# Samples' B and C in the state-space scan: spread over partitions by the tensor engine, or by a transfer through DRAM

## The reference

```python
state_new = state * exp(dt * a) + (dt * x)[:, None] * B[None, :]      # per head: 64 x 128
y = (state_new * C[None, :]).sum(-1) + d_skip * x
```

## Time and profile before

| | |
|---|---|
| median of 3 runs | 1481.87 us |
| profiled execution, its own time | 1483.19 us |
| its span in the trace | 1481.4 us |
| PE busy | 1396.4 us (94%) |
| DVE busy | 858.4 us (58%) |
| ACT busy | 568.1 us (38%) |
| POOL busy | 608.5 us (41%) |
| mean granted clock of TensorE | 0.97 |
| moved by DMA | 160.47 MB, mean 108 GB/s |

### The profile page before, as it was taken

The page is one execution under the profiler, slowest core; times in us unless marked ns, Lnnn a source line. Parts: engine busy times, 40 slices in busy tenths (PEclk is TensorE's granted clock), DMA queues, the critical chain, the costliest instruction groups (busy, mean ns, idle before and its releaser), DMA issues.

```text
span 1481.4 us, 28721 instructions
## 1 busy us (share of the span) xinstructions
PE 1396.4 (94%) x11570; PEld 1301.2 (88%) x11570; DVE 858.4 (58%) x1713; ACT 568.1 (38%) x1162; POOL 608.5 (41%) x753
## 2 busy tenths in 40 slices
PE   4998999999999999999999999999489999999994
PEld 4997898998989889898898877899479999999994
DVE  6477878878788787887876534233542222222226
ACT  3344544544545354444445222222233322233221
POOL 4442352433525335352423322445435454544541
PEclk9999999999999999999999999899779999999997
DMA  4222222322222232232334899433012223232231
GB/s 160 86 79 89 83 79 72 103 90 81 85 89 89 86 92 76 86 94 72 93 113 119 253 358 356 143 130 101 29 57 89 94 90 100 86 98 89 86 100 58
DMA packets 109588, 160.47 MB, mean 108 GB/s; under 512 B 16496, under 2 KB 83568, under 8 KB 109456
## 3 DMA queue, kind: packets, MB, share of 16 engines
q1 hardware_dynamic: 54864, 127.32, 27.2%
q10 hardware_dynamic: 54592, 31.33, 7.2%
HBM read 145.87 MB, written 12.74 MB: 107 GB/s over the span
## 4 chain that ended last, share of the span: by engine, by line
PE 66%; DVE 15%; ACT 4%; SPq 3%; issue 2%; DMA 1%; POOL 1%; ACTq 0%; DVEq 0%; POOLq 0%
PE lin L523 52%; SPq L400 2%; PE lin L730 2%; DVE arena L1528 1%; PE Pb L685 1%; PE Pb L556 1%; PE lin L626 1%; DVE arena L1691 1%; DVE ysum L1694 1%; ACT arena L1173 1%; PE Pb L669 1%; DVE sm L1613 1%; DMA w_stage<-in_wall 1%; PE Pb L678 1%; DVE arena L1621 1%
## 5 line engine op out<-in xcount | busy, mean ns | idle before, releaser
L471 POOL TENSOR_TENSOR w_lo<-w_stage,w_hi 128x256 fp32r<-128x256 f32 x736 | 587.7, 830 | 815.9 <-ACT w_hi L968 815.9
L523 PE MATMUL lin<-act_hi,w_hi 128*128 128x260 f32 x1760 | 367.1, 290 | 12.4 <-DVEq L1693 4.3
L523 PE MATMUL lin<-act_lo,w_hi 128*128 128x260 f32 x1760 | 357.0, 285 | 0.0
L523 PEld LDWEIGHTS lin<-act_hi,w_hi 128*128 128x128 f32 x1760 | 274.1, 191 | 26.9 <-issue 22.0
L523 PEld LDWEIGHTS lin<-act_lo,w_hi 128*128 128x128 f32 x1760 | 275.4, 191 | 0.0
L968 ACT ACTIVATE w_hi<-w_stage 128x1024 fp32r<-128x1024 f32 x184 | 193.5, 1052 | 200.2 <-PE lin L523 154.7
L523 PE MATMUL lin<-act_hi,w_lo 128*128 128x260 f32 x1760 | 236.0, 287 | 0.0
L523 PEld LDWEIGHTS lin<-act_hi,w_lo 128*128 128x128 f32 x1760 | 222.3, 191 | 0.0
L523 PE MATMUL lin<-mid_hi,w_hi 128*128 128x260 f32 x1008 | 206.5, 286 | 1.1 <-issue 1.1
L523 PE MATMUL lin<-mid_lo,w_hi 128*128 128x260 f32 x1008 | 203.9, 284 | 0.0
L523 PEld LDWEIGHTS lin<-mid_hi,w_hi 128*128 128x128 f32 x1008 | 157.6, 191 | 2.7 <-issue 2.3
(11 more groups left out here) (265 smaller groups left out, 1879.0 us busy)
## 6 DMA issues: line engine op xcount, KB each, us to landing
w_stage<-in_wall SPq DMA_DIRECT2D x184, 512.0 KB, 3.6
arena<-in_cache ACTq DMA_DIRECT2D x80, 144.0 KB, 4.4
arena<-in_state ACTq DMA_DIRECT2D x16, 512.0 KB, 5.1
out_stateT<-arena ACTq DMA_DIRECT2D x16, 512.0 KB, 4.1
o_attn<-in_cache SPq DMA_DIRECT2D x64, 128.0 KB, 4.3
arena<-in_cache SPq DMA_DIRECT2D x64, 128.0 KB, 4.1
arena<-in_cache SPq DMA_DIRECT2D x48, 144.0 KB, 4.2
arena<-in_xT SPq DMA_DIRECT2D x8, 520.0 KB, 5.5
```

The costliest lines, as they stand in the source:

```text
L471: low = pool.tensor_tensor(w_lo[:, slot, part], w_stage[:, slot, part], w_hi[:, slot, part].bitcast(F32), ALU.subtract)
L523: mm = pe.matmul(lin[:, pl.slot, hf, 0:HALF], w[:, ch.slot, off:off + P], r[:, hf * HALF:(hf + 1) * HALF], start=(k == 0 and p == 0), stop ...
```

## The change

B and C of the samples no longer pass through the tensor engine. DVE copies the 8 sample columns of `xc` (128 partitions x 8) into a small tile `smp` (`samples_apart`); ACT's queue writes it to a DRAM buffer of [8, 128], which takes one 4-byte piece for each of 1024 numbers (`samples_out`); when that has landed, ACT's queue reads the 4 KB back to each of the 128 partitions (`samples_in`), B into `sga_mid`, C into a part of the convolution's buffer. DVE waits for `b_in` and `c_in` and takes both operands of its products from SBUF. The entries bB and bC leave the list of slots. B and C of group i's inputs are written and read back at the end of group i; those of group 0 are read back in block 0 of group 1, where the state update now stands after `raw_samples(1)`, `sample_y(0)` after `scan_back(0)` and `sample_y(1)` in block 1.

```diff
--- before.py
+++ after.py
@@ -50,12 +50,12 @@
 S_LIN = [f"s{m}" for m in range(8)]
 FIRST_LIN = ["x0", "x1", "bcq", "b", "c", "bckv", "z0", "z1", "uq0", "uq1", "uk", "uv", "ql"]
 FIRST_CONV = [3, 0, 1, 2]
-STEADY_LIN = (["bB", "x0", "sA0", "x1", "bC", "sA1", "b", "sA2", "c", "sA3", "z0", "z1", "uq0", "uq1", "uk", "uv", "ql"]
+STEADY_LIN = (["x0", "sA0", "x1", "sA1", "b", "sA2", "c", "sA3", "z0", "z1", "uq0", "uq1", "uk", "uv", "ql"]
               + S_LIN)
 EARLY = 6
 OA_ORDER = [0, 1, 2, 3, 4, 7, 5, 6]
 OA_BEFORE = [0, 2, 4, 5, 6]
-LAST_LIN = (["bB", "ga0", "sA0", "ga1", "bC", "sA1", "ga2", "sA2", "ga3", "sA3", "ga4", "ga5", "ga6"] + S_LIN)
+LAST_LIN = (["ga0", "sA0", "ga1", "sA1", "ga2", "sA2", "ga3", "sA3", "ga4", "ga5", "ga6"] + S_LIN)
 FIRST_CH = IN_LIN + ["UQ", "UKV"]
 STEADY_CH = IN_LIN + ["UQ", "UKV", "SA", "SB"]
 LAST_CH = [f"ga{k}" for k in range(EARLY + 1)] + ["SA", "SB"]
@@ -121,7 +121,7 @@
     return fixed(CH_D + GATES_BEFORE[b] + q)
 
 
-C_LIN = [FIRST_LIN, ["x0", "bB"] + STEADY_LIN[2:]] + [STEADY_LIN] * 6 + [LAST_LIN]
+C_LIN = [FIRST_LIN] + [STEADY_LIN] * 7 + [LAST_LIN]
 
 
 def c_lin(i, name):
...
+    sdec_mm sdec_ready st_in0 st_in1 st_scaled smp_ready smp_out0 smp_out1 b_in c_in st_new st_out0 st_out1 scores max_bias exp_done prob_ready
...
@@ -235,6 +235,7 @@
         snb = sb("snb", [P, 3])
         sga_mid = sb("sga_mid", [P, 2, T])
         sm = sb("sm", [P, 8])
+        smp = sb("smp", [P, 2, NB])
         sms = sb("sms", [P, 8])
         ahead = sb("ahead", [SSM_HEADS, 1])
 
@@ -270,7 +271,7 @@
         sz = part(4 * T, "p (k t) -> p k t", k=4)
         yT = part(2 * T, "p (k t) -> p k t", k=2)
         state = part(256)
-        sT = arena[:, at[0]:at[0] + 2048].rearrange("p (t b n) -> p t b n", t=2, b=NB)
+        sT = arena[:, at[0]:at[0] + 1024].rearrange("p (b n) -> p b n", b=NB)
         sqg = arena[:, at[0]:at[0] + 2 * T].rearrange("p (k t) -> p k t", k=2)
         seg = part(512, "p (h l) -> p h l", h=HPG)
         ecs = part(512, "p (h l) -> p h l", h=HPG)
@@ -323,6 +324,13 @@
         sq2 = part(KT * T, "p (k t) -> p k t", k=KT)
         relu = part(2 * T + 68)[:, 68:].rearrange("p (k t) -> p k t", k=2)
         sqsum = part(T, "p (k t) -> p k t", k=1)
+
+        sT_first = o_attn[:, 6:8, :].rearrange("p k t -> p (k t)").rearrange("p (b n) -> p b n", b=NB)
+        B_all = sga_mid[:, :, :].rearrange("p k t -> p (k t)")[:, 0:NB * STATE]
+
+        def C_all(g):
+            a = early + 2 * T if g == GROUPS - 1 else early + 2 * T - 4 * CONVW + NB * STATE
+            return arena[:, a:a + NB * STATE]
 
         def sz_of(i, k):
             return sz[:, 2 * (i % 2) + k, :]
@@ -721,28 +729,15 @@
                     pe.wait_ge(S["cs_split"], 1)
                     first_scores()
                     project(0)
-                pe.wait_ge(S["xc_ready"], g * 4 + 4)
-
-                def on_all(name, k):
-                    pl = c_lin(i, name)
-                    free_slot(pl)
-                    for b in range(NB):
-                        mm = pe.matmul(lin[:, pl.slot, b // 4, (b % 4) * P:(b % 4 + 1) * P],
-                                       xc[:, k, SAMP0 + 4 * b:SAMP0 + 4 * b + 1].to_broadcast([P, P]), ident[:, :],
-                                       start=True, stop=True)
-                    mm.then_inc(S["lin_done"], 1)
-
-                on_all("bB", 2)
                 if g:
                     first_scores()
                     project(0)
+                pe.wait_ge(S["xc_ready"], g * 4 + 4)
                 for c in range(NCH):
                     u = 2 * c
                     scan_front(c)
                     scores(u + 1)
                     project(c + 1, between=lambda: transposes(u))
-                    if c == 0:
-                        on_all("bC", 3)
                     values(u)
                     transposes(u + 1)
                     scan_back(c)
@@ -1073,6 +1068,19 @@
                         scaled = act.activation(sS[:, t, b, :], sS[:, t, b, :], ACT.Identity,
                                                 scale=sdec_all[:, i, t, 8 + b:9 + b])
                     scaled.then_inc(S["st_scaled"], 1)
+
+                def samples_out(t):
+                    act.wait_ge(S["smp_ready"], i * 2 + t + 1)
+                    act.dma_start(o["samples"][i, t].rearrange("b n -> n b"), smp[:, t, :], allow_slow_non_contiguous=True).then_inc(S[f"smp_out{t}"], 16)
+
+                def samples_in(t, i=i):
+                    act.wait_ge(S[f"smp_out{t}"], i * 16 + 16)
+                    if t == 0:
+                        act.wait_ge(S["st_new"], i * 2)
+                    else:
+                        act.wait_ge(S["xc_ready"], i * 4 + 4)
+                    act.dma_start((B_all, C_all(i))[t], o["samples"][i, t].rearrange("b n -> (b n)").partition_broadcast(P)
+                                  ).then_inc(S[("b_in", "c_in")[t]], 16)
 
                 def queries_out(h):
                     pl = c_lin(i, f"uq{h}")
@@ -1132,6 +1140,8 @@
                     conv_tanh(2)
                     conv_tanh(3)
                     act.wait_ge(S["rows_ready"], 1)
+                    for t in range(2):
+                        samples_out(t)
                     return
 
                 def exponent(u):
@@ -1166,6 +1176,9 @@
                         act.wait_ge(S["state_ready"], g * 4 + c)
                     act.activation(Brow[:, :], lin[:, pl.slot, 1, 256:384], ACT.Copy).then_inc(S["a_row"], 1)
                     exponent(u + 1)
+                    if i == 1 and c == 0:
+                        for t in range(2):
+                            samples_in(t, 0)
                     act.wait_ge(S["a_seg"], g * 4 + (c + 1))
                     act.activation(ecs[:, :, :], lin[:, pl.slot, 0, :].rearrange("p (h l) -> p h l", h=HPG),
                                    ACT.Exp).then_inc(S["a_ecs"], 1)
@@ -1238,7 +1251,12 @@
                     conv_tanh(3)
                     scaled_state(0)
                     scaled_state(1)
+                    samples_out(0)
                 round_chunk(c_chunk(i, "SB").next())
+                if has_in:
+                    samples_in(0)
+                    samples_out(1)
+                    samples_in(1)
 
             group(0)
             for i in range(1, GROUPS):
@@ -1535,6 +1553,13 @@
                     dve.wait_ge(S["conv_tanh"], i * 4 + (n + 1))
                     dve.scalar_tensor_tensor(xc[:, k, :], xc[:, k, :], 1.0, cacc[:, k, :], ALU.add, ALU.mult
                                              ).then_inc(S["xc_ready"], 1)
+                    if has_rest and k >= 2:
+                        samples_apart(k - 2)
+
+                def samples_apart(t):
+                    dve.wait_ge(S[f"smp_out{t}"], i * 16)
+                    dve.wait_ge(S["xc_ready"], i * 4 + (3 + t if has_rest else 4))
+                    dve.tensor_copy(smp[:, t, :], xc[:, 2 + t, SAMP0:CONVW:4]).then_inc(S["smp_ready"], 1)
 
                 def queries_out(h):
                     pl = c_lin(i, f"uq{h}")
@@ -1605,6 +1630,8 @@
                     conv(3)
                     silu(2)
                     silu(3)
+                    samples_apart(0)
+                    samples_apart(1)
                     return
 
                 def row_max(u):
@@ -1666,31 +1693,27 @@
                 if g == 0:
                     row_max(0)
                     raw_samples(0)
-                dve.wait_ge(S["xc_ready"], g * 4 + 4)
-                dve.wait_ge(S["st_scaled"], g * 2 + 2)
-                link(dve.tensor_tensor(dtx[:, :, :], sdec_all[:, g, :, 0:8], xc[:, 0:2, SAMP0:CONVW:4], ALU.mult))
-                pl = c_lin(i, "bB")
-                bB = lin[:, pl.slot, :, :].rearrange("p a (b n) -> p (a b) n", b=4)
-                done(pl)
-                link(dve.tensor_tensor(sT[:, 0], bB, spread(dtx[:, 0, :], STATE), ALU.mult))
-                dve.tensor_tensor(sT[:, 1], bB, spread(dtx[:, 1, :], STATE), ALU.mult).then_inc(S["lin_free"], 1)
-                dve.wait_ge(S["lin_free"], pl.index + 1)
-                for t in range(2):
-                    dve.tensor_tensor(sS[:, t], sS[:, t], sT[:, t], ALU.add).then_inc(S["st_new"], 1)
-                    dve.wait_ge(S["st_new"], g * 2 + (t + 1))
+
+                def sample_states():
+                    dve.wait_ge(S["xc_ready"], g * 4 + 4)
+                    dve.wait_ge(S["st_scaled"], g * 2 + 2)
+                    link(dve.tensor_tensor(dtx[:, :, :], sdec_all[:, g, :, 0:8], xc[:, 0:2, SAMP0:CONVW:4], ALU.mult))
+                    dve.wait_ge(S["b_in"], g * 16 + 16)
+                    for t in range(2):
+                        new = sT if g else sT_first
+                        link(dve.tensor_tensor(new, B_all.rearrange("p (b n) -> p b n", b=NB), spread(dtx[:, t, :], STATE),
+                                               ALU.mult))
+                        dve.tensor_tensor(sS[:, t], sS[:, t], new, ALU.add).then_inc(S["st_new"], 1)
```

(23 more changed lines are left out.)

1 line of the change is left out of this document (removed).

## The result

The kernel after takes 1606.91 us (median of 4 runs, 1601.97 to 1609.84) against 1482.38 for the kernel before, measured with it: ratio 1.0835 [1.0814, 1.0856], slower by some 124 us. The forecast was 1489, in a range that ended at 1508. The direction was right and the size far off. The profiled execution of after took 1601.97 us with a span of 1600.2, which is 118.8 more than before's 1481.4.

What follows compares the result with a forecast made beforehand. PE and DVE were taken as nearly tied, with DVE holding PE at each group's stretch end. Steady groups +6, group 8 0, group 1 +1.4 sum to 7.4 us, giving 1489 against the median 1481.87; range 1472 to 1508.

Steps and rivals of the forecast that it cites:

- I take 4.0: Landing of B's write in 4-byte pieces in steady groups: 4.0 us, between 2.3 from below and 6.5 from above.
- this wait costs nothing as long as R is 403, with 2 us to spare: ACT's wait for the landings before history, x1's rounding and x0's copy in steady groups: no cost, 2 us of room.
- R: Point in a group when DVE frees x0's slot: 401.01 before in group 4, forecast 403.0, 2.0 us later.
- Rival 2: Long round trip: write lands in 6.5, broadcast in 5.1, ACT's two landings in series; +28 us, 1510; chance 0.22.
- lands at 398.4 + 2.3 = 400.7, hidden as well: History load in a steady group: issued at 398.4, lands 2.3 us later, before it is needed, at no cost.
- Steady groups: Groups 2 to 7: +2.0 us up to R, -1.0 after it, +1.0 each, +6 us together.
- Group 1: States move later in the same block, extra ACT issues and DVE copies, slot waits go: +1.4 us.
- Group 8: Later states mostly fit in the 2.79 us gap left by a late weight chunk: +1 - 1 = 0.
- The tie: From about 400 to 434 in each group PE and DVE nearly tied, DVE holding PE at the end of that stretch.
- Two at 1.59: Four state operations of DVE per steady group, now from SBUF: two at 1.22, two at 1.59 us; 5.7 in all.
- Rival 3: DVE's chain gives way, so PE's removed work counts: 1446 at most, half of it 1464; chance 0.08.
- Rival 1: Short round trip: both landings together 5.9 us, below the 7.1 balance; steady groups gain, 1476, faster; chance 0.18.

Runs made afterwards that it cites:

- e4: Against the kernel after: only samples 0 to 3 written and read (512 pieces of 4 B side by side), samples 4 to 7 reuse them; 1600.88 us, ratio 1.0770.
- e10: Against the kernel after: the 1024 pieces of 4 B lie 64 bytes apart, reads take 4 KB of the weights instead; 1492.18 us, ratio 1.0046.
- e2: Against the kernel after: C's read, with its wait for the write, moved behind the second exponent of the next group's first block; 1597.12 us, ratio 1.0756.
- e5: Against the kernel before: DVE's copies and the 4-byte writes added, nobody reads them, B and C stay on PE; 1520.37 us, ratio 1.0235.
- e8: Against the kernel before: only C moved through DRAM, in 8-byte pieces, read back in block 0; B stays on PE; 1488.53 us, ratio 1.0027.
- e1: Against the kernel after: buffer not transposed, 128 pieces of 32 B, DVE reads with a step of 8; 1511.97 us, ratio 1.0190.
- e9: Against the kernel after: four samples per piece, 256 pieces of 16 B, DVE reads with a step of 4; 1515.59 us, ratio 1.0204.

## Why the prediction was wrong

**What failed: "I take 4.0", with 6.5 as the upper end, for the write in 4-byte pieces.** It was taken from the rows nearest in size, writes and loads whose pieces are of 128 bytes and more, and from the state loads, which have the same number of pieces. Measured: 10.9 median and 9.0 at least, above the upper end in every one of 16 writes. Number and size of the pieces were what the bounds were made of, and neither sets this landing (e4, e10); what does is that 4-byte pieces lie side by side, and no row of before has that. A bound "from above" by another kind of transfer was none.

**The sentence that followed, "this wait costs nothing as long as R is 403, with 2 us to spare", fell with it.** In group 4 ACT's series takes 21.9 us from the first write's issue to `history`, and R waits for it. Rival 2 had this mechanism ("ACT's two landings in series set R, each further us costs 2 per group") and priced it with 6.5. By its rule 10.9 gives 4.0 + 2 x 3.9 = 11.8 per steady group; measured 15.2. So the mechanism was foreseen, with a chance of 0.22 and too small a price.

**The rest: the history load "lands at 398.4 + 2.3 = 400.7, hidden as well".** It is last in the series and not hidden: it takes 4.3, and DVE waits 3.47 for it at R. Behind unfinished small writes it takes 11.4 (e2) or 14 (e5). After R the clock takes 1.3 that the sum had not.

**By term of the sum.** Steady groups: +6 forecast, +91.4 measured. Group 1: +1.4 forecast, +9.2 measured (PE waits 10.79 at x1 and 2.98 at L686). Group 8: 0 forecast, since the late B would "fit in most of this gap" of 2.79; PE waits 15.40 there, and from group 8's start on the kernel takes 18.1 longer.

**What held.** The tie: removed products pay next to nothing (e8). The stretch after R: 32.5 forecast; in e10, where the waits are short, R is 410.72 and `normalise` ends at 442.38 + 0.90, 32.6. The steady groups without the slow landing: e10's write lands in 3.5, its reads in 4.1 and 5.0, near the assumed 4.0 and 4.1, and groups 2 to 7 take 3.4 us more than in before, where the sum had 6. The timeline of ACT in e10, as forecast with "393.2, 393.8, 397.8, 398.4" relative to 389.17:

```profile
397.57 0.37 ACTq L1074 DMA_DIRECT2D samples<-smp  x1
...
400.44 0.35 ACTq L1082 DMA_DIRECT2D sga_mid<-in_wall  x1
401.31 0.37 ACTq L1074 DMA_DIRECT2D samples<-smp  x1
405.28 0.35 ACTq L1082 DMA_DIRECT2D arena<-in_wall  x1
405.72 0.59 ACTq L1018 DMA_DIRECT2D arena<-in_hist  x1
```
```profile
410.72 0.17 DVE L1511 COPY arena<-lin 128x8 f32<-128x8 f32 x1 [0.64 <-DMA arena<-in_hist]
```

Write to R is 13.2 there; the forecast had 403.0 - 389.17 = 13.8. Even here it is the history load, not DVE's states, that R waits for at the end, so the 2 us to spare were not there either.

**What agrees by luck.** e10 as a whole takes 8.2 us more than the kernel before beside it (1492.18 - 1484.0), and the sum said 7.4. Its terms do not agree. The profiled execution of e10 is longer by 14.2: 3.4 in the steady groups, 3.8 in group 1 (1.4 forecast) and 8.0 from the start of group 8 on (0 forecast). PE waits there in e10:

```profile
PE lin L531 <- DVE arena L1511: 15.0, 8, 3.3
...
PE lin L531 <- DVEq L1524: 6.2, 1, 6.2
```

The second is group 8. Its two weight chunks are issued within 0.7 us of the read of C and land in 8.3 and 9.1 us; in before, without that read, they land in 4.4 and 5.2. The sum counted the gap that a late chunk leaves as room for the states, and not that the added read moves at the same time as the chunk.

**Smaller terms.** "Two at 1.59": with B this late POOL ran beside none of them, and all four state operations of group 4 took 1.22 or 1.23; `sample_y(0)` took 1.73 against the assumed 1.59. "No L730, PE's busy time down by about 31": it fell by 4.4, because the waits cost clock; no term had that. Rival 3 is out: no run with the spreading products gone came out faster than the kernel before. Rival 1's condition, under 7.1 us for both landings, holds for B in e1 (median 1.8, read 3.6) and e9 (2.3, read 4.4), where the stepped reads take the gain back, and narrowly in e10 (2.7, read 4.1), where DVE reads as in after; e10's steady groups are no faster than before's. Whether landings of 5.9 would win isn't settled.

**The count of the pieces.** Packets under 512 B went from 16496 to 33392, 16.9 thousand more for 16 writes of 1024 numbers. So the count agrees with the Trainium skill, DMA: Bandwidth & Descriptors, "Rules for kernel authors" (a strided last dimension becomes one descriptor per element). Its fit in "Anatomy of one DMA", 2.0 us plus the bytes over 436 GB/s and measured on another path, gives 2.0 for this write, an estimate by that page; 10.9 was measured, and the measurement decides. The same page, "Specifications", says that a transfer below 512 B is done by read-modify-write. That would fit neighbours that have to wait for one another, but by itself it says the same of e1, e10 and after (2.0, 3.5, 10.9), and no run here shows the mechanism.
